# A float32 two-block model on one core: the first of three split products of every feed-forward up piece widened to 512 columns, and small moves around it

## The reference

```
# first block, layer 0 (attention) and layer 1 (recurrent)
for layer in range(2):
    h = h + mixer(rmsnorm(h, norm_mix[layer]))
    z = relu(rmsnorm(h, norm_mlp[layer]) @ w1[layer])      # 1024 -> 4096
    h = h + (z * z) @ w2[layer]                            # 4096 -> 1024
h = rmsnorm(h, norm_final)
# second block
def swiglu(x): return (silu(x @ w_gate) * (x @ w_up)) @ w_down   # 1024 -> 2816 -> 1024
h = h + 0.5 * swiglu(rms_norm(h, ffn1_norm))
h = h + concat(window_attention, multiscale_pool)(rms_norm(h, mix_norm) @ w_in) @ w_out
h = h + 0.5 * swiglu(rms_norm(h, ffn2_norm))
out = rms_norm(h, final_norm)
```

## Time and profile before

| what | value |
|---|---|
| runs | 1043.33, 1044.7, 1045.14 us (median 1044.7) |
| profiled execution, device time | 1045.01 us |
| its span in the trace | 1043.2 us |
| granted clock of PE over it | 0.999 |
| busy: PE, DVE, ACT, POOL | 1029.8, 667.3, 489.3, 42.8 us |
| instructions: PE, DVE, ACT | 6965, 816, 599 |
| HBM read | 182.62 MB, 176 GB/s over the span |

### The profile page before, as it was taken

The page is one execution under the profiler, slowest core; times in us unless marked ns, Lnnn a source line. Parts: engine busy times, 40 slices in busy tenths (PEclk is TensorE's granted clock), DMA queues, the critical chain, the costliest instruction groups (busy, mean ns, idle before and its releaser), DMA issues.

```text
span 1043.2 us, 16367 instructions
## 1 busy us (share of the span) xinstructions
PE 1029.8 (99%) x6965; PEld 946.1 (91%) x6965; DVE 667.3 (64%) x816; ACT 489.3 (47%) x599; POOL 42.8 (4%) x41
## 2 busy tenths in 40 slices
PE   9999999999999999999999999999999999999997
PEld 6899899999999979999999999999998889999996
DVE  4587576665667797655556765655577666556554
ACT  6455463443436865343343644334356553444342
POOL 1200010000001301000000200000010010000000
PEclk9999999999999999999999999999999999999999
DMA  9863436556553446665665576465643245664621
GB/s 326 272 220 106 142 122 208 196 174 195 197 169 115 162 152 227 206 202 163 201 195 169 187 247 201 165 202 163 200 161 113 91 127 199 220 202 162 202 82 41
DMA packets 121734, 184.74 MB, mean 177 GB/s; under 512 B 3081, under 2 KB 100541, under 8 KB 121535
## 3 DMA queue, kind: packets, MB, share of 16 engines
q1 hardware_dynamic: 119504, 176.70, 51.9%
q0 software_dynamic: 1696, 6.41, 1.7%
q10 hardware_dynamic: 462, 0.60, 0.2%
HBM read 182.62 MB, written 1.07 MB: 176 GB/s over the span
## 4 chain that ended last, share of the span: by engine, by line
PE 92%; DVE 4%; ACT 2%; issue 1%; DMA 0%; POOL 0%; DVEq 0%; POOLq 0%; ACTq 0%
PE bank L1342 34%; PE bank L1318 17%; PE bank L1320 17%; PE bank L1321 17%; DVE w_lo L693 2%; PE bank L1489 2%; PE bank L1368 1%; PE bank L1475 1%; PE bank L1462 1%; DMA work<-in_vectors 0%; PE bank L1463 0%; PE bank L1649 0%; PE bank L1513 0%; ACT w_hi L357 0%; PE bank L1651 0%
## 5 line engine op out<-in xcount | busy, mean ns | idle before, releaser
L693 DVE TENSOR_TENSOR w_lo<-raw,w_hi 128x2048 fp32r<-128x2048 f32 x165 | 377.0, 2290 | 182.0 <-ACT w_hi L357 182.0
L1318 PE MATMUL bank<-xT_hi,w_hi 128*128 128x256 f32 x1520 | 435.0, 286 | 0.0
L1321 PE MATMUL bank<-xT_hi,w_lo 128*128 128x256 f32 x1520 | 429.9, 283 | 0.0
L1320 PE MATMUL bank<-xT_lo,w_hi 128*128 128x256 f32 x1520 | 429.9, 283 | 0.0
L357 ACT ACTIVATE w_hi<-raw 128x2048 fp32r<-128x2048 f32 x165 | 313.9, 1909 | 92.6 <-PE bank L1342 84.9
L1318 PEld LDWEIGHTS bank<-xT_hi,w_hi 128*128 128x128 f32 x1520 | 291.2, 192 | 3.2
L1320 PEld LDWEIGHTS bank<-xT_lo,w_hi 128*128 128x128 f32 x1520 | 291.3, 192 | 2.3
L1321 PEld LDWEIGHTS bank<-xT_hi,w_lo 128*128 128x128 f32 x1520 | 291.1, 192 | 0.0
L1342 PE MATMUL bank<-w_hi,z_hi 128*128 128x512 f32 x472 | 153.2, 394 | 2.2 <-DVE w_lo L693 1.3
L1342 PE MATMUL bank<-w_lo,z_hi 128*128 128x512 f32 x472 | 151.4, 390 | 0.0
L1342 PE MATMUL bank<-w_hi,z_lo 128*128 128x512 f32 x472 | 151.1, 390 | 0.0
(11 more groups left out here) (205 smaller groups left out, 748.0 us busy)
## 6 DMA issues: line engine op xcount, KB each, us to landing
raw<-in_w SPq DMA_DIRECT2D x64, 1024.0 KB, 5.4
raw<-in_f_gate SPq DMA_DIRECT2D x22, 1024.0 KB, 5.4
raw<-in_f_up SPq DMA_DIRECT2D x22, 1024.0 KB, 5.4
raw<-in_f_down SPq DMA_DIRECT2D x22, 1024.0 KB, 5.0
raw<-in_w_in SPq DMA_DIRECT2D x13, 1024.0 KB, 5.3
raw<-in_w_qkv SPq DMA_DIRECT2D x10, 1024.0 KB, 9.2
raw<-in_w_o SPq DMA_DIRECT2D x4, 1024.0 KB, 5.7
raw<-in_rec_w_o SPq DMA_DIRECT2D x4, 1024.0 KB, 5.1
```

What stands on the lines that cost most here:

```text
L693: e.tensor_tensor(w_lo[n % RING], raw[n % RAW], r32(w_hi[n % RING]), ALU.subtract).then_inc(lo_done, 1)
L1318: e.matmul(o, whi[:, k, cut], xT_hi[:, k, :], start=(k == 0 and b == 0), stop=False, skip_group_check=True)
L1320: e.matmul(o, whi[:, k, cut], xT_lo[:, k, :], start=False, stop=False, skip_group_check=True)
L1321: last = e.matmul(o, wlo[:, k, cut], xT_hi[:, k, :], start=False, stop=(k == KB - 1), skip_group_check=True)
```

## The change

In the feed-forward stages alone, xT becomes one tile in which block k holds hi and lo side by side. `u_wide` (in place of `u_block`) multiplies w_hi once by both, 512 columns, and w_lo by xT_hi, 256 columns, into one bank for each half of the piece. The sum of hi·lo stands in the bank's right half, and has to be added to the left half: ACT copies the right half to `low` (`low_leaves`, two copies of 128 x 256 for each piece), DVE adds the left half to it (`sums`, two adds of 128 x 256 for each piece). A piece now needs two banks: in gated stages banks 4 and 5 for gate and 6 and 7 for up, in plain ones the pairs alternate. The `zeros` products that open banks 0 to 3 move behind `z_ready(0)`, and a gated spread goes to bank 1, later than before.

In plain stages `rms` is no longer applied to u: relu(u)² is taken with rstd left out, and `down_scale` = 1/var (rstd squared) is applied in `add`; `diags`, `spread` and the copy of rms fall away there, and so does POOL's rstd. In gated stages `down_scale` is 0.5·rstd: up is no longer multiplied by rms.

The last stage runs one more part of its second last down piece ahead of the wait for the last z, and its last token tile 0 is closed in halves. Small moves elsewhere: `KEEP` from 11 to 6; ACT's `hi(3)` ahead of an Exp that waits for DVE; `hi(8)` and `lo(8)` earlier in the QK pieces; `lo(F2's second)` and a copy earlier in X2's out stage, and PE's turning and applying of its attention weights one place earlier each.

```diff
-WARM, KEEP = 26, 11
+WARM, KEEP = 26, 6
+SPREAD = {j: i + 1 for i, j in enumerate((L0, L1, F1, X2, F2))}
+SCALED = {L1: 1, F1: 2, X2: 3}
+    def banks(self, p, i):
+        b = 4 + 2 * (p % 2 if self.nu == 1 else i)
+        return b, b + 1
...
-    xT_hi, xT_lo = sb("xT_hi", [P, KB, S], F32R), sb("xT_lo", [P, KB, S], F32R)
+    xT = sb("xT", [P, KB, 2, S], F32R)
+    xT_hi, xT_lo = xT[:, :, 0, :], xT[:, :, 1, :]
... 
# ACT
+        def low_leaves(f, p, i):
+            e.wait_ge(used, f.ups(p) + i + 1)
+            if f.sums(p, i) > 1:
+                e.wait_ge(z_sum, 2 * f.sums(p, i) - 2)
+            for b, n in enumerate(f.banks(p, i)):
+                e.activation(low[:, b * S:(b + 1) * S], bank[n][:, S:2 * S], ACT.Copy).then_inc(z_low, 1)
         def gate(f, p):
+            if p:
+                low_leaves(f, p, 0)
             e.wait_ge(z_g, f.g0 + p - G_NU2 + 1)
             e.activation(tmp[0], tmp[0], ACT.Silu).then_inc(z_s, 1)
         def feed_forward(f, beside=None):
+            if f.nu == 2:
+                low_leaves(f, 0, 0)
             hi(f.n0 + LOOK)
             if f.nu == 2:
-                hi(f.n0 + 1 + LOOK)
                 if f.j == F1:
                     normed_squares()
+                low_leaves(f, 0, 1)
+                hi(f.n0 + 1 + LOOK)
                 gate(f, 0)
...
+        hi(3)
         e.wait_ge(sp_step, 2)
         e.activation(sp[2], sp[1], ACT.Exp).then_inc(sp_exp, 1)
-        for n in (3, 4):
-            hi(n)
+        hi(4)
... 
# DVE
+        def sums(f, p, i, t):
+            e.wait_ge(used, f.ups(p) + i + 1)
+            for b, n in enumerate(f.banks(p, i)):
+                e.wait_ge(z_low, 2 * f.sums(p, i) - 1 + b)
+                here = slice(b * S, (b + 1) * S)
+                e.tensor_tensor(t[:, here], bank[n][:, 0:S], low[:, here], ALU.add).then_inc(z_sum, 1)
+            e.wait_ge(z_sum, 2 * f.sums(p, i))
         def z_finish(f, p):
             if f.nu == 1:
                 t, z = tmp[0], tmp[1]
+                sums(f, p, 0, t)
...
-                e.scalar_tensor_tensor(out=pair(t), in0=pair(src), scalar=0.0, in1=rms_pair(), op0=ALU.max,
-                                       op1=ALU.mult).then_inc(z_t, 1)
-                e.wait_ge(z_t, g_ + 1)
-                e.tensor_tensor(z, t, t, ALU.mult).then_inc(z_f, 1)
+                e.scalar_tensor_tensor(out=z, in0=t, scalar=0.0, in1=t, op0=ALU.max, op1=ALU.mult).then_inc(z_f, 1)
             else:
                 g, u, z = tmp
-                e.tensor_tensor(pair(u), pair(src), rms_pair(), ALU.mult).then_inc(z_t, 1)
+                if p:
+                    sums(f, p, 1, u)
...
# PE
+        def u_wide(n, k, banks):
...
+            for b, i in enumerate(banks):
+                cut = slice(b * P, (b + 1) * P)
+                e.matmul(bank[i], whi[:, k, cut], xT[:, k, :, :].rearrange("p b s -> p (b s)"), start=(k == 0),
+                         stop=False, skip_group_check=True)
+                last = e.matmul(bank[i][:, 0:S], wlo[:, k, cut], xT_hi[:, k, :], start=False, stop=(k == KB - 1),
+                                skip_group_check=True)
+            return last
...
                 for i in range(f.nu):
-                    if p >= f.bufs:
-                        e.wait_ge(z_g if f.nu == 2 and i == 0 else z_t,
-                                  f.g0 + p - f.bufs + 1 - (G_NU2 if f.nu == 2 and i == 0 else 0))
...
+                    before = p - 2 if f.nu == 1 else p - 1
+                    if before >= 0:
+                        e.wait_ge(z_sum, 2 * f.sums(before, i))
+                    u_piece(f.ups(p) + i, f.banks(p, i), between if i == 0 else None, u_wide)
...
-                ups(p, {3: lambda: spread(f.j)} if p == 1 else None)
+                ups(p, {7 if f.j == F1 else 4: lambda: spread(f.j)} if p == 1 and f.nu == 2 else None)
+                z_ready(p - 1)
                 if p == 1:
                     for i in range(4):
                         e.matmul(bank[i][:, 0:2], zeros, zeros[:, 0:2], start=True, stop=False, skip_group_check=True)
-                z_ready(p - 1)
                 d_piece(f.down(p - 1), from_z((p - 1) % f.bufs))
...
                 d_part(*one, 0, (0, 1), (0, 1))
+                d_part(*one, 1, (0, 1), (0,))
                 z_ready(p)
                 split(two[0])
-                d_part(*two, 0, (0, 1), (0, 1), last=True).then_inc(last_closed, 1)
-                closing_tokens(one, two, last_closed)
+                for half in range(2):
+                    d_part(*two, 0, (0, 1), (half,), last=True).then_inc(last_closed, 1)
+                closing_tokens(one, two, last_closed, (1,))
...
+        turn_weights(a2, 3, 0)
         e.wait_ge(mix_lo, 13)
         apply_weights(a2, 2)
...
         d_part(*one, 0, (0, 1), (0,))
-        turn_weights(a2, 3, 0)
+        turn_weights(a2, 3, 1)
         d_part(*one, 1, (0, 1), (0,))
-        turn_weights(a2, 3, 1)
+        apply_weights(a2, 3)
         d_part(*one, 0, (0, 1), (1,))
-        apply_weights(a2, 3)
+        heads_to_xT(a2, 1, bank[4])
         d_part(*one, 1, (0, 1), (1,)).then_inc(used, 1)
-        heads_to_xT(a2, 1, bank[4])
         e.wait_ge(mix_lo, 14)
         closing(two, F2)
```

More of the change, by code:

```diff
@@ L236, in build @@
     MIX_BANK = {0: 0, 1: 2, 4: 0}
+    spread_bank = {L0: bank[7], L1: bank[7], F1: bank[1], X2: bank[7], F2: bank[1]}
     a_ = vec("a_param")
@@ L740, in turn @@
             lo(n_next - 1 + LOOK)
-            if j != F1:
+            if j in SPREAD and j != F1:
                 diags(j)
         def spread(j):
-            e.wait_ge(spread_done, j + 1)
-            e.tensor_copy(rms, bank[7][:, 0:S]).then_inc(rms_done, 1)
-        def gate(f, p):
-            e.wait_ge(used, f.ups(p) + 1)
-            if p == 0:
-                e.wait_ge(rms_done, f.j + 1)
-            e.tensor_tensor(pair(tmp[0]), pair(bank[4 + p % f.bufs * 2]), rms_pair(), ALU.mult).then_inc(z_g, 1)
+            e.wait_ge(spread_done, SPREAD[j])
@@ new lines, in spread @@
+            e.tensor_copy(rms, spread_bank[j][:, 0:S]).then_inc(rms_done, 1)
+        def sums(f, p, i, t):
[5 more added lines that the diff above has]
+            e.wait_ge(z_sum, 2 * f.sums(p, i))
+        def gate(f, p):
+            if p:
+                sums(f, p, 0, tmp[0])
+            else:
+                e.wait_ge(rms_done, SPREAD[f.j])
+            e.tensor_tensor(pair(tmp[0]), pair(tmp[0]), rms_pair(), ALU.mult).then_inc(z_g, 1)
@@ L798, in feed_forward @@
         def feed_forward(f, beside=None):
-            if f.j == F1:
-                normed_h()
+            if f.nu == 2:
+                sums(f, 0, 0, tmp[0])
+                if f.j == F1:
+                    normed_h()
             lo(f.n0 + LOOK)
-            if f.j == F1:
-                normed_variance()
             if f.nu == 2:
+                if f.j == F1:
+                    normed_variance()
+                sums(f, 0, 1, tmp[1])
                 lo(f.n0 + 1 + LOOK)
-            if f.j == F1:
-                both_rstds()
-                diags(F1)
-            spread(f.j)
-            if f.nu == 2:
+                if f.j == F1:
+                    both_rstds()
+                    diags(F1)
+            if f.nu == 1:
+                e.wait_ge(var_done, f.j + 1)
+                e.reciprocal(down_scale, var).then_inc(scale_done, 1)
+            else:
+                spread(f.j)
+                e.tensor_scalar(down_scale, rstd, 0.5, None, ALU.mult).then_inc(scale_done, 1)
                 gate(f, 0)
```

102 lines of the change are left out of this document (51 added, 51 removed).

## The result

| | before | changed |
|---|---|---|
| median, us | 1044.91 (1043.33 to 1045.14, 4 runs) | 1032.2 (1030.77 to 1032.27, 4 runs) |
| profiled execution, its span | 1045.01, 1043.2 | 1030.77, 1029.0 |
| ratio | | 0.9883, 95% interval 0.9871 to 0.9895 |

The kernel is faster by 12.7 us, 1.17%. The forecast was 1025, with a range from 1021.5 to 1032, so the time lies just above the range.

What follows compares the result with a forecast made beforehand. PE's own stream was taken as the kernel's length. Terms 15.8 + 0.9 + 0.4 + 3.9 - 0.3 - 0.9 - 0.3 = 19.5 us off 1045.0 gave 1025.5, stated as a median of 1025, range 1021.5 to 1032.

Steps and rivals of the forecast that it cites:

- The product: Up and gate pieces: 512 plus 256 columns replace three products of 256, 0.013 us less a block, 1216 blocks, 15.8 us.
- a rival of 7%: Block gets no cheaper: the short product waits for its weights, 512 + 256 takes the old 0.360; 1041 us, chance 0.07.
- The rule of the Trainium skill: A warm product costs its columns at 2.4 GHz plus about 2.5 ns; 3.0 us saved in place of 15.8.
- The spreads: M0 and M1 lose their spreads, 0.45 us each in the chain: 0.9 us gained.
- M0's and M1's closings: Copies and adds push `hi` and `lo` back at both closings: 0.15 us lost each, 0.3 together; above, 0.6 each.
- F1's closing and entry: Closing: 0.4 us wait for z, later adds to h, 0.9 lost; entry: later diags and spread, 0.3 lost.
- F2's gain: F2's closing: six more products stand before the wait for the last z; 0.4 us gained, bounds 0 and 0.4.
- Small moves: `KEEP` 1.0, `hi(3)` 1.0, QK pieces 0.7 and X2's out stage 1.2: 3.9 us gained.
- the start: Fewer products of zeros (`KEEP`) let the first true product start earlier: 1.0 us gained, bounds 0 and 1.6.
- Second best, 1031: The product pays, but edges cost their upper ends and about half the moves are lost; 13.6 us gained, chance 0.19.
- wait for `z_sum`: Sign of the slower rival: PE waits in front of gate pieces for DVE's queue; 1052 us, chance 0.03.
- the head: Everything until L0's closing, with the moves at the start, `hi(3)` and the QK pieces: 2.7 us gained.

Runs made afterwards that it cites:

- both long: Changed kernel with w_lo too multiplied by xT's hi and lo, so both products of a block have 512 columns: 1151.64 us (one run).
- three short: Changed kernel with only the width undone, three products of 256 columns with three weight loads: 1039.21 us, ratio to before 0.9957.
- pairs in one bank and in two: Changed kernel with two long products, then two short: all four to one bank 1025.32 us (one run), over two banks 1024.88 us.

## Why the prediction was wrong, point by point

- **The product.** This is the step that failed: "I take 0.013, and keep 0 as an end", with the reason that a thinner stream of weight loads is the easier one. The distances of 0.120 and 0.227 were read in rows of equal products, and added up for a stream in which they alternate. In that stream the long product takes 0.236, the short one 0.117 and the block 0.3527: 0.0070 us saved, 8.5 us and not 15.8. With 8.5 in the sum the forecast would have been 1032.5. The two pure streams do hold their distances (experiments with both long and with three short), and the saving of 0.013 is nearly there when the order is long, long, short, short: 0.0117 a block in double pieces. The mechanism was right, its size in this order was not, and the bound below, 0, was taken for a rival of 7% when it should have widened the range of the term. And it is only half true that the mixed stream was not in the trace: two products in turn are not, but 46 places where long ones follow short ones are, with 234, 236, 228, 232 and 231 ns before 227, and the reading of 0.227 began just behind one of them, at 204.44. They would not have given 0.3527 (the first distances alone, 234 and 113, add up to 0.347 again), but they show that a distance depends on what went before.
- **The rule of the Trainium skill** (page "TensorE: Matmul & The Clock Gate", section "Wait — 56ns, not 53.3ns?"), 3.0 us for the products saved, came out too low: three short products against long and short in turn are 7.0 us by the medians, 8.5 by the block. The measured 7.0 ns a block lies between the page's 2.5 and the 13 of the rows. The products of zeros at the start (bf16, 512 columns, with a load each too) do agree with the page: 216 ns apart, 2 to 3 over their columns at 2.4 GHz. It is the float32 ones that stand 227 apart.
- **The spreads** gave what was forecast or a little more: M0 in the kernel with three short products gains 0.8 and M1 0.5, against 0.45 each less 0.15. What the rest of M0's gain is stays open.
- **Edges.** M0's and M1's closings cost nothing to be seen; F1's closing and entry, forecast at 1.2, cost about 0.6: 0.1 for z, where 0.4 was forecast, 0.4 for the transposes that wait for h, where half a us was (the table has it in X2), and 0 to 0.1 for the entry. The two copies and two adds in a row were charged at 0.9 and 0.85 and took 0.66 and 0.75. F2's gain, 0.4, is there (0.5).
- **Small moves**: 4.9 by the traces against 3.9; the start gave 1.7 where 1.0 was taken (bound 1.6), `hi(3)` 1.15 for 1.0, the QK pieces 0.9 for 0.7, the out stage 1.35 for 1.2. Part of this is luck of the profiled run: with zeros at the longer distance L0 gains 2.8 to 3.6 us and not 3.7.
- **What no term had**: the clock. The fall behind L1's gap costs 0.6 us, in six of eight runs if the mean clock is a sign of it; the longer distance in the first products costs up to 0.9 (L0's closing at 128.49 and 129.39). The profiled run has neither, so it is the fastest of its four; together they are of the size of the 1.5 us between profile and median, but how they stand in the three other runs is not shown. The same kernel on another chip had 1031.27.
- **Rivals.** Second best, 1031, has the nearest number, but for another reason: its edges were to cost 5.1 and half the moves to be lost, and neither came; what did not pay in full is the product. That the time is near 1031 is luck. No wait for `z_sum` came up.

In one sum: 19.5 forecast, less 7.3 for the product, plus 1.0 for the head, plus 1.5 for spreads and edges of the feed-forward stages (9.8 gained there less 8.5, where -0.2 was forecast), less 0.3 in L1 and X2 (moves of 1.35 less F1's 0.4) make 14.4, against 14.3 measured.

## What to carry to other kernels

A distance from start to start holds for the stream in which it was read. When a change mixes two kinds of products, look for places in the trace where one kind follows the other, down to the first few distances behind the change, and give the term the whole range from no gain to the full one; then try the order: same products, same bytes, long, long, short, short in place of long, short gave 6 us more, where the wide product itself gave 8. Moves that bring a just-in-time operand forward were the safe part: each gave its wait.

## What the hardware showed that was not expected

- After short products (256 columns, float32, each with its own weight load), long ones (512) start 233, 236, 228, 233 and 231 ns apart before they are back at 227; the short ones behind long ones start 113 and 119 ns apart and then at 120. It has nothing to do with the bank that is written (pairs in one bank and in two, 5.564 and 5.563 us a piece), nor with the operands (the down pieces of the kernel before show it too). What in the engine keeps this account stays open: no run here separates the weight loads from the products.
- PE idle for 1.1 us after 366 was followed by 3.4 us at the lower clock (1.2 GHz) in one of two profiles of the changed kernel and in five of eleven of all kernels with that gap. It did not come in the two profiles with the gap filled with products of zeros, nor in that of the kernel before, which has a gap of 1.1 us there at 372.
- At the start the clock rises at a different time from run to run: products of zeros of 512 columns stand 0.427 us apart in eight profiles with six of them and 0.216 in the profile of the changed kernel, and the end of L0 moves by up to 0.9 us with it.
